# The delta mixer's key and value layers computed by Strassen's scheme, the convolution moved between their products, attention's steps put at fixed places, and PSUM units asked for when they are first written

## The reference

```
qkv = silu(causal_conv(gqkv, conv_w))          # 4 taps along time, per channel
q, k = l2norm(query heads), l2norm(key heads)  # 8 heads of 128
g = -exp(a_log) * softplus(ga + dt_bias); beta = sigmoid(gb)
o = gated_delta_rule(q, k, v, g, beta)
o = rmsnorm(o) * gdn_gn * silu(gz)
```

## Time and profile before

| | us |
|---|---|
| median of 3 runs | 2909.76 |
| the profiled execution's own time | 2909.25 |
| its span in the trace | 2907.5 |
| TensorE products busy | 2757.1 (95%) |
| TensorE weight loads busy | 2410.0 (83%) |
| VectorE busy | 1353.6 (47%) |
| ScalarE busy | 480.6 (17%) |
| GpSimd busy | 170.6 (6%) |
| DMA read | 472.64 MB, 163 GB/s over the span |

### The profile page before, as it was taken

One profiled execution on the slowest core, in us unless ns is written; L12 is line 12 of the kernel. 1 busy time (PEld: TensorE's weight loads), 2 busy tenths in 40 slices (PEclk: granted clock), 3 DMA queues, 4 the chain that ended last, 5 costly groups with the idle time before them and its releaser, 6 DMA issues.

```text
span 2907.5 us, 40974 instructions
## 1 busy us (share of the span) xinstructions
PE 2757.1 (95%) x18154; PEld 2410.0 (83%) x18154; DVE 1353.6 (47%) x1844; ACT 480.6 (17%) x767; POOL 170.6 (6%) x155
## 2 busy tenths in 40 slices
PE   8999899999999989899999999899799989987998
PEld 5768788999686878899998878695699988766998
DVE  5443223895645232533330000157568767576454
ACT  1251110101126111110010000023111011212110
POOL 0002210000000321000000000000000010000000
PEclk9999999999999999999999999999799989998999
DMA  7432214884443212244445888634169634332442
GB/s 262 145 116 87 73 58 167 324 318 173 144 159 130 73 58 73 105 175 166 167 153 182 291 287 291 212 119 160 58 252 358 223 112 136 132 116 87 160 160 88
DMA packets 211920, 476.34 MB, mean 164 GB/s; under 512 B 7584, under 2 KB 36896, under 8 KB 211488
## 3 DMA queue, kind: packets, MB, share of 16 engines
q1 hardware_dynamic: 211168, 472.26, 46.6%
q10 hardware_dynamic: 576, 1.46, 0.1%
HBM read 472.64 MB, written 1.05 MB: 163 GB/s over the span
## 4 chain that ended last, share of the span: by engine, by line
PE 81%; issue 11%; DVE 6%; ACT 2%; DMA 1%; POOL 1%; SPq 0%; POOLq 0%; DVEq 0%; ACTq 0%
PE ps L460 21%; PE ps L1645 17%; PE ps L518 7%; PE ps L2154 7%; PE ps L526 7%; PE ps L1840 5%; PE ps L1886 4%; PE ps L2183 3%; PE ps L1146 1%; PE ps L1157 1%; PE ps L1153 1%; PE ps L2193 1%; PE ps L731 0%; PE ps L2126 0%; DVE ring L609 0%
## 5 line engine op out<-in xcount | busy, mean ns | idle before, releaser
L460 PE MATMUL ps<-uT,ring 128*128 128x256 f32 x1792 | 403.8, 383 | 18.5 <-DMA ring<-in_w_in 9.3
L460 PEld LDWEIGHTS ps<-uT,ring 128*128 128x128 f32 x1792 | 339.6, 192 | 66.9 <-issue 11.1
L2154 PEld LDWEIGHTS ps<-work,ring 128*128 128x128 f32 x1760 | 198.6, 192 | 5.1 <-issue 4.8
L2154 PE MATMUL ps<-work,ring 128*128 128x128 f32 (+4 forms) x1760 | 198.4, 275 | 0.0
L1645 PE MATMUL ps<-uT,ring 128*128 128x128 f32 x1584 | 190.0, 279 | 3.2 <-ACT uT L889 2.5
L1645 PEld LDWEIGHTS ps<-uT,ring 128*128 128x128 f32 x1584 | 186.1, 196 | 5.3 <-issue 5.0
L460 PE MATMUL ps<-xn,ring 128*128 128x256 f32 x768 | 175.1, 387 | 9.5 <-issue 6.9
L1645 PE MATMUL ps<-xn,work 128*128 128x128 f32 x1584 | 179.8, 275 | 0.0
L1645 PEld LDWEIGHTS ps<-xn,work 128*128 128x128 f32 x1584 | 178.3, 192 | 0.0
L460 PEld LDWEIGHTS ps<-xn,ring 128*128 128x128 f32 x768 | 147.3, 195 | 31.1 <-issue 11.3
L1690 ACT ACTIVATE work<-ps 128x512 f32<-128x512 f32 (+1 forms) x108 | 60.3, 559 | 418.1 <-PE ps L1645 418.1
(11 more groups left out here) (457 smaller groups left out, 4331.7 us busy)
## 6 DMA issues: line engine op xcount, KB each, us to landing
ring<-in_w_in SPq DMA_DIRECT2D x72, 1024.0 KB, 5.1
work<-in_ada_w SPq DMA_DIRECT2D x48, 1024.0 KB, 10.7
ring<-in_exp_w_down SPq DMA_DIRECT2D x40, 1024.0 KB, 5.2
ring<-in_attn_w_in SPq DMA_DIRECT2D x36, 1024.0 KB, 5.2
ring<-in_exp_w_gate SPq DMA_DIRECT2D x32, 1024.0 KB, 6.2
ring<-in_exp_w_up SPq DMA_DIRECT2D x32, 1024.0 KB, 7.4
ring<-in_ffn_w_in SPq DMA_DIRECT2D x32, 1024.0 KB, 7.5
ring<-in_ffn_w_out SPq DMA_DIRECT2D x22, 1024.0 KB, 8.6
```

The lines of the kernel that those rows point to most:

```text
L460: mm = pe.matmul(acc[:, m * T:(m + 1) * T], w[:, k, m * P:(m + 1) * P], src[:, half * 4 + k, :], start=(half == 0 and k == 0 and m % 2 == ...
L2154: mm = pe.matmul(acc[:, m * c:(m + 1) * c], w[:, k, m * P:(m + 1) * P], picked[:, half * 4 + k, OFFS[i]:OFFS[i] + c], start=(half == 0 and ...
```

## The change

1. The slab list loads key (`gk`) and value (`gv`) in the order of a quad; only the query's 1024 columns stay linear.
2. `quad_phases_pe` gets `slots=None`. Without slots both units are taken before P4 as before; with slots the first is asked for (and waited for) at P4, the second at P1.
3. `mixer_tail_pe`: the second query half layer, then gk, gv and gz as quads with named units, the four norm sums at named phases of them (behind P1 and P6 of gk, P5 of gv, P5 of gz) and the decay product behind P4 of gz.
4. ScalarE and VectorE follow: the additions of gk and gv write into the convolution's input buffers `cin`, ScalarE makes the last tap from `cin` in SBUF, and the convolution of each half layer is done during the next layer's phases.
5. `attention_order` places the steps of groups 0 and 1 at named phases of the next group's query and key layers and none in its value layer; for group 2 the first two steps stand behind P5 and P3 of its value layer, the rest behind P7. VectorE's last two rotations (group 2, key) come before the sums of its value layer. The quads use the pair of units that the preceding norm's broadcast does not use.

```diff
@@ -266,7 +266,9 @@
-        linear(f"gqkv{l}", w, OFF_GQKV, 3072)
+        linear(f"gqkv{l}", w, OFF_GQKV, D)
+        quad(f"gk{l}", w, OFF_GQKV + D)
+        quad(f"gv{l}", w, OFF_GQKV + 2 * D)
@@ -492,15 +494,17 @@
-                   slots=(None, None)):
+                   slots=None):
...
-    u1 = take_unit(pe, f"{slab}1", slots[0])
-    u0 = take_unit(pe, f"{slab}0", slots[1])
+    if slots is None:
+        u1, u0 = take_unit(pe, f"{slab}1"), take_unit(pe, f"{slab}0")
+    else:
+        u1, u0 = ps[slots[0]], ps[slots[1]]
@@ -533,6 +537,8 @@
+        if slots is not None and what in ("P4", "P1"):
+            take_unit(pe, slab + "10"[what == "P1"], slots[what == "P1"])
@@ -1028,27 +1034,43 @@
-def mixer_tail_pe(pe, l):
-    for j in range(6):
-        if j:
-            linear_t(pe, f"gqkv{l}", f"gqkv{l}{j}")
-        if j < 2:
-            continue
-        pe.wait_ge(sq_out, 4 * l + j - 1)
-        acc = take_unit(pe, f"nrm{l}{j - 2}")
-        for i in range(2):
-            mm = pe.matmul(acc[:, i * 512:(i + 1) * 512], ones, sq[j % 2][:, i * 512:(i + 1) * 512],
-                           start=True, stop=True)
-        mm.then_inc(tick(psum_full), 1)
-    acc = take_unit(pe, f"ab{l}")
+def norm_sum_pe(pe, l, j, slot):
+    pe.wait_ge(sq_out, 4 * l + j + 1)
+    acc = take_unit(pe, f"nrm{l}{j}", slot)
+    for i in range(2):
+        mm = pe.matmul(acc[:, i * 512:(i + 1) * 512], ones, sq[j % 2][:, i * 512:(i + 1) * 512],
+                       start=True, stop=True)
+    mm.then_inc(tick(psum_full), 1)
+def decay_pe(pe, l, slot):
+    acc = take_unit(pe, f"ab{l}", slot)
...
-    quad_pe(pe, f"gz{l}", True)
+def mixer_tail_pe(pe, l):
+    linear_t(pe, f"gqkv{l}", f"gqkv{l}1")
+    s = [(slot_of[f"gqkv{l}1"] + 1 + i) % 4 for i in range(4)]
+    for what, phase in quad_phases_pe(pe, f"gk{l}", False, slots=(s[0], s[1])):
+        phase()
+        if what == "P1":
+            norm_sum_pe(pe, l, 0, s[2])
+        if what == "P6":
+            norm_sum_pe(pe, l, 1, s[3])
+    for what, phase in quad_phases_pe(pe, f"gv{l}", False, slots=(s[2], s[3])):
+        phase()
+        if what == "P5":
+            norm_sum_pe(pe, l, 2, s[0])
+    for what, phase in quad_phases_pe(pe, f"gz{l}", True, slots=(s[0], s[1])):
+        phase()
+        if what == "P4":
+            decay_pe(pe, l, s[3])
+        if what == "P5":
+            norm_sum_pe(pe, l, 3, s[2])
+    next_slot[0] = s[2]
@@ -1195,40 +1217,52 @@
-    for j in range(6):
+    for j in range(2):
...
-        n = 6 * l + j
-        if j >= 3:
-            root_act(act, l, j - 3)
...
-        if j >= 2:
-            act.wait_ge(conv_acc, n - 1)
-            act.wait_ge(conv_out, n - 1)
...
-        w = col(f"conv{l}")
-        for a in range(4):
-            i_ = act.activation(cacc[j % 2][:, a, :], acc[:, a * T:(a + 1) * T], ACT.Copy,
-                                scale=w[:, (4 * j + a) * 4 + 3:(4 * j + a) * 4 + 4])
-        i_.then_inc(tick(conv_in), 1)
+        last_tap_act(act, l, j, acc[:, :].rearrange("p (a t) -> p a t", a=4)).then_inc(tick(conv_in), 1)
...
-        if j >= 1:
-            conv_silu(act, l, j - 1)
-        if 1 <= j <= 4:
-            square_act(act, l, j - 1)
-    root_act(act, l, 3)
-    conv_silu(act, l, 5)
+    conv_silu(act, l, 0)
+    square_act(act, l, 0)
+    gk, gv, gz = f"gk{l}", f"gv{l}", f"gz{l}"
+    conv_snaps = snap_buffers(0)
+    quad_snaps(act, gk, conv_snaps, ("P4", "P1"))
+    conv_silu(act, l, 1)
+    square_act(act, l, 1)
+    root_act(act, l, 0)
+    quad_snaps(act, gk, conv_snaps, ("P5", "P6"))
+    root_act(act, l, 1)
+    conv_tap_act(act, l, 2, gk)
+    conv_tap_act(act, l, 3, gk)
+    quad_snaps(act, gv, conv_snaps, ("P4", "P1"))
+    conv_silu(act, l, 2)
+    square_act(act, l, 2)
+    quad_snaps(act, gv, conv_snaps, ("P5", "P6"))
+    root_act(act, l, 2)
+    conv_silu(act, l, 3)
+    square_act(act, l, 3)
+    conv_tap_act(act, l, 4, gv)
+    conv_tap_act(act, l, 5, gv)
+    quad_snaps(act, gz, conv_snaps, ("P4",))
...
+    quad_snaps(act, gz, conv_snaps, ("P1",))
+    conv_silu(act, l, 4)
...
-    quad_snaps(act, f"gz{l}", snap_buffers(0))
-    quad_done(act, f"gz{l}")
+    quad_snaps(act, gz, conv_snaps, ("P5", "P6"))
+    root_act(act, l, 3)
+    conv_silu(act, l, 5)
+    quad_done(act, gz)
@@ -1263,6 +1297,20 @@
+def last_tap_act(act, l, j, src):
+    w = col(f"conv{l}")
+    for a in range(4):
+        i_ = act.activation(cacc[j % 2][:, a, :], src[:, a, :], ACT.Copy,
+                            scale=w[:, (4 * j + a) * 4 + 3:(4 * j + a) * 4 + 4])
+    return i_
+def conv_tap_act(act, l, j, slab):
+    n = 6 * l + j
+    act.wait_ge(conv_acc, n - 1)
+    act.wait_ge(conv_out, n - 1)
+    act.wait_ge(q_out, 4 * quad_no[slab] + 2 * (j % 2) + 2)
+    last_tap_act(act, l, j, cin[j % 2][:, :, 3:259]).then_inc(tick(conv_in, 2), 2)
@@ -1356,10 +1404,8 @@
-    for j in range(6):
+    def conv_taps(j):
...
-        if j >= 3:
-            unit_norm(j - 3)
@@ -1370,13 +1416,41 @@
-    unit_norm(3)
-    quad_sums_dve(dve, f"gz{l}", 0)
-    quad_sums_dve(dve, f"gz{l}", 1)
+    gk, gv, gz = f"gk{l}", f"gv{l}", f"gz{l}"
+    conv_dst = [c[:, :, 3:259] for c in cin]
+    def add(slab, *which):
+        for w in which:
+            if slab != gz and w[1] == "1":
+                dve.wait_ge(conv_acc, 6 * l + 2 * (slab == gv) + int(w[0]))
+            quad_add_dve(dve, slab, w, snap_buffers(0), o_gdn if slab == gz else conv_dst)
+    conv_taps(0)
+    conv_taps(1)
+    for part in range(3):
+        quad_sums_dve(dve, gk, part)
+    add(gk, "11")
+    quad_sums_dve(dve, gk, 3)
+    unit_norm(0)
+    add(gk, "12", "21", "22")
+    conv_taps(2)
+    for part in range(3):
+        quad_sums_dve(dve, gv, part)
+    unit_norm(1)
+    quad_sums_dve(dve, gv, 3)
+    conv_taps(3)
+    add(gv, "11", "12", "21", "22")
+    quad_sums_dve(dve, gz, 0)
...
+    conv_taps(4)
+    for part in range(1, 4):
+        quad_sums_dve(dve, gz, part)
@@ -1387,10 +1461,11 @@
-    quad_sums_dve(dve, f"gz{l}", 2)
-    quad_sums_dve(dve, f"gz{l}", 3)
-    for which in ("11", "12", "21", "22"):
-        quad_add_dve(dve, f"gz{l}", which, snap_buffers(0), o_gdn)
+    unit_norm(2)
+    conv_taps(5)
+    add(gz, "11", "12")
+    unit_norm(3)
+    add(gz, "21", "22")
@@ -2852,18 +2927,20 @@
-    layers = [phases(g, 0) + phases(g, 1) + phases(g, 2) for g in range(3)]
-    seq = list(layers[0])
+    seq = phases(0, 0) + phases(0, 1) + phases(0, 2)
+    beside = {0: {"P1": "s1", "P2": "t0", "P6": "s2 t1", "P3": "o0", "P7": "s3"},
+              1: {"P4": "t2", "P5": "o1", "P6": "t3", "P3": "o2", "P7": "o3"}}
...
-        nxt = layers[g + 1][:21 if g == 0 else 18]
-        for i, (w, pr) in enumerate(steps_):
-            seq.append((w, g, pr, None))
-            n = (i + 1) * len(nxt) // len(steps_) - i * len(nxt) // len(steps_)
-            for k in range(n):
-                seq.append(nxt[i * len(nxt) // len(steps_) + k])
-    P6, P3, P7 = layers[2][18:]
-    own = [(w, 2, pr, None) for w, pr in steps_]
-    return seq + own[0:1] + [P6] + own[1:2] + [P3] + own[2:4] + [P7] + own[4:]
+        seq.append(("s", g, 0, None))
+        for which in range(2):
+            for step in phases(g + 1, which):
+                seq.append(step)
+                seq += [(w[0], g, int(w[1]), None) for w in beside[which].get(step[3], "").split()]
+        for step in phases(g + 1, 2):
+            seq.append(step)
+            if g == 1 and step[3] in ("P5", "P3"):
+                seq.append(("s", 2, ("P5", "P3").index(step[3]), None))
+    return seq + [(w, 2, pr, None) for w, pr in steps_[2:]]
@@ -2881,10 +2958,11 @@
-    ready, slot = {}, [2]
+    quad_slot = 2 if slot_of["rbsmix1"] < 2 else 0
+    ready, slot = {}, [2 - quad_slot]
...
-        slot[0] = 5 - slot[0]
+        slot[0] = 2 * (2 - quad_slot) + 1 - slot[0]
@@ -2892,7 +2970,7 @@
-                ready = dict(quad_phases_pe(pe, f"at{g}{j}", j == 2, sums=at_sums, slots=(1, 0), **first))
+                ready = dict(quad_phases_pe(pe, f"at{g}{j}", j == 2, sums=at_sums, slots=(quad_slot + 1, quad_slot), **first))
@@ -3017,16 +3095,19 @@
+                if (g, j) == (2, 2):
+                    turn_rope(g, 2)
+                    turn_rope(g, 3)
...
-                if j:
+                if j and (g, j) != (2, 2):
...
-                if j:
+                if j and (g, j) != (2, 2):
...

```

## The result

The changed kernel takes 2881.95 us (median of 4 runs, 2879.05 to 2882.25), the one before in the same comparison 2911.89 (4 runs, 2909.72 to 2923.24): a ratio of 0.9886, 95% interval 0.9864 to 0.9908. Forecast were 2877, between 2868 and 2889. Its profiled execution took 2882.01 (span 2880.2 against 2907.5), so in the traces the change is worth 27.3 us where the sum had 32.5. Over all comparisons of this study the runs of the kernel before fall into two groups, 23 between 2908.95 and 2914.02 us and 14 between 2916.87 and 2923.24, while all 14 of the changed kernel lie between 2878.97 and 2882.32; the first trace of before is from the lower group, and a ratio of medians depends on how many of its runs fell in the upper one.

What follows compares the result with a forecast made beforehand. TensorE was taken as the bound, 81% of the chain. 10.0 us from both mixers and 22.5 from attention, 32.5 off 2909.25, gave 2876.8, stated as 2877 with the median's 0.5; range 2868 to 2889.

Steps and rivals of the forecast that it cites:

- Key and value layers: Mixer: key and value as 14 products of 3.57 us, 49.98 instead of 55.24; 5.26 saved per mixer.
- The rule of the Trainium skill: Mixer's key and value: weight load and product would add up, 14 products taking 100 us; the prediction rejected it.
- The gate layer: Mixer's gate layer: P6 wait of 1.59 goes, slow product behind the decay product stays at 1.78.
- The mixer's end: Behind the gate's P7 (209.9): v transposes wait 1.2 for a SiLU; first Gram product at 219.8; 5.0 gained per mixer.
- Units late, steps at fixed places: Attention: P4's unit waits go, 7.4; moved steps remove 7.05 and 7.8; 22.0 after 0.3 back.
- The start: Attention's first product starts 2.0 us earlier with the other pair of units; bounds 0 and 2.4.
- The tail behind the last P7: Attention's end: VectorE work moved behind P7 adds 4.8; TensorE's 1.96 moves there too and is hidden.
- The step that was off: Attention's layer 22: both rotations before the sums make the first sum late for P5, 0.3 us back.
- A: Mixer: VectorE does convolutions ahead of sums, five products per mixer wait 1.5 us each; 2892 us; chance 0.08.
- B: Attention: steps find new waits, half of the two big stalls' 14.9 us comes back; 2884.2 us; chance 0.08.
- D: Attention: late asking gains nothing, ScalarE's copy of P4 waits for the same addition; 7.4 lost, 2884.2 us; chance 0.02.
- C: Gate layer: low clock behind the decay product slows six products, 37.7 us in all; 2914.5 us; chance 0.03.

Runs made afterwards that it cites:

- experiment 1: Against the kernel before, new mixers with old attention: 2902.65 us, ratio 0.9968. Against the changed kernel, both units asked for at P4: 2886.54; attention's old order: 2891.18.

## Why the prediction was right, step by step

- **Key and value layers**: 14 products in 50.01 (49.98 forecast), no wait for a ring sum. The least slack, the value's first sum, was done at 161.24 for a P5 at 163.21: 1.97 where 2.0 was laid out. The last tap from SBUF took 1.71 (1.56 taken, 4 needed to show). The rule of the Trainium skill that was weighed (TensorE: Matmul & The Clock Gate, "The mechanism", the section before the one that the prediction names) does not fit these layers: they load and multiply in 3.57 per 32 pairs again, and adding up would have cost 50 us more per mixer.
- **The gate layer**: right in its size by two terms that weren't separate. The wait at P6 (1.59) and the slow product (1.78) were counted as one that goes and one that stays. The second trace of before shows that the wait covered the slow product: the sum's time did not depend on it. So the change took the cover away, and what the product costs now (1.7 per mixer, in 11 of 18) it did not cost before. "Its bounds are 0 and 1.78 per mixer" held.
- **The mixer's end**: P7 ended at 210.25 (209.9 forecast, for an entry 0.35 earlier), the wait before the v transposes was there (0.99), the first Gram product came at 219.98 (219.8). Per mixer 5.3 and 5.65 (5.0 forecast) where the gate layer has its slow product, as forecast, 10.9 in the trace of experiment 1; 7.0 where it has none.
- **Units late, steps at fixed places**: the order is worth 10.5 and asking late 4.8 in it. The 7.4 of the prediction were those of the old order; with late asking the old order is 8.2 faster than without (297.61 to 289.45), the other pair of units included. The start gave 2.05 (2.0), the end 1.3. The tail behind the last P7 grew from 19.5 to 22.7 us (2585.39 to 2608.14), by 3.3 where the sum has 4.8 less the 1.3 of the end. The "some 275" for attention's length is a slip: 297.66 less the 20.5 that the sum takes out behind the start is 277.2; measured are 278.5 and 279.0.
- **The step that was off** is the smallest term: "The first sum is then done some 11 us after P7 of layer 21, and P5 wants it at 10.6: 0.3 back". P5 waited 1.72. The two rotations were priced at 2 x 3.66 from a row in which GpSimd stood still; now the first begins 0.77 into GpSimd's product of 2.35 for the same rotation and takes 1.44 more. That is 1.4 more than the 0.3 of the sum, and attention's shortfall is 1.3 (21.2 instead of 22.5); that every other term was right to the tenth does not follow.
- **The rest of the 5 us**: outside the change, in stretches at the low clock that both kernels have in some traces (2.7 in the HGRN, 0.5 to 1.9 between the mixers). The HGRN's is in the second trace of before too. By medians the change is worth 29.9 in the first comparison, 30.1 in that of experiment 1 and 36.7 in the last, where more runs of before were long. The sum's starting point was a profiled execution of 2907.5 that happened to miss every one of the slow stretches of the second trace, at 2919.9. That the forecast came within 5 us is therefore in part luck: taken off the second trace's 2921.72, the same 32.5 would have given 2889, the edge of the range.
- The rivals: A, B and D are excluded by the rows and experiment 1; C did not happen, the clock was back after one product each time.

## What to carry to other kernels

Price an operation of VectorE by a row in which GpSimd does what it will do beside the moved one. Take a second trace of the kernel before, and see which stretches repeat, ahead of adding up tenths. Before a stall is counted as gain and a slow stretch beside it as cost, ask whether the one covered the other. And when a rotation of buffers is shifted, follow it to the next place that names a buffer by number: two waits of 3.1 us removed here came back as one of 5.6 and a low clock, 200 us later.

## What the hardware showed

In these traces a VectorE operation with both inputs in SBUF took longer beside a GpSimd operation: L952 3.88 to 4.51 instead of 2.44, a sum of ring slabs 3.37 instead of 2.28, a convolution 5.79 instead of 5.09 beside a copy of 2.42. Work with an input in PSUM did not: in the changed kernel a scaling step (L3144, 2556.98) took its usual 0.69 inside the L943 that began at 2556.93. The granted clock behind the 16-column run was 0.72 from 186 to 192 us in one execution of the changed kernel and 1.00 from 187 to 193 in the next, which had reached the place 1.1 us later; the HGRN's fell in 9 of 14 traces. Two traces of one kernel were 12.4 us apart, most of it at lower clocks; a forecast from one trace carries that as an error.
